# A norm vector's load and a weight split moved at two seams of a two-block transformer kernel on one Trainium2 core

## The reference, cut to what matters

```python
for i in range(DEPTH):                                   # DEPTH = 2
    h = rms_norm(x, norm1_g[i]) * (1.0 + sc1) + sh1
    x = x + g1 * attention_i(h)                          # begins with h @ w_in: (512 x 1024) @ (1024 x 3072)
    h = rms_norm(x, norm2_g[i]) * (1.0 + sc2) + sh2
    y = hierarchical_moe(h, ...)                         # each token: 2 of 32 experts, weighted
    x = x + g2 * y
x = rms_norm(x, final_norm_g)                            # final norm of the first block
# second block: h = x; for l in range(DEPTH): h = h + hybrid_mixer(rms_norm_2(h, norm_mix[l]), ...) ...
#   hybrid_mixer begins with xn @ w_in[l]
```

## Time and profile before

| | us |
|---|---|
| median of 3 runs (2644.32 to 2647.06) | 2645.24 |
| the profiled execution, whole | 2640.27 |
| its span, first to last instruction | 2638.2 |
| PE busy in it | 2262.7 |
| DVE busy | 1091.4 |
| ACT busy | 591.2 |
| POOL busy | 292.3 |

### The profile page before, as it was taken

The page is one execution under the profiler, slowest core; times in us unless marked ns, Lnnn a source line. Parts: engine busy times, 40 slices in busy tenths (PEclk is TensorE's granted clock), DMA queues, the critical chain, the costliest instruction groups (busy, mean ns, idle before and its releaser), DMA issues.

```text
span 2638.2 us, 34590 instructions
## 1 busy us (share of the span) xinstructions
PE 2262.7 (86%) x12932; PEld 1477.3 (56%) x12932; DVE 1091.4 (41%) x1953; ACT 591.2 (22%) x1157; POOL 292.3 (11%) x518
## 2 busy tenths in 40 slices
PE   4998686898977679996988887775998999999997
PEld 2874374453433368653554443343787765787764
DVE  2237744333333342654323233335327615227614
ACT  3114521000000031541000000003336214336213
POOL 0000111212121110000212122112000000000000
PEclk9999897999999989998999999997999799999799
DMA  6247827999999832115999999995211021121021
GB/s 243 96 154 312 344 100 312 420 420 420 419 420 420 354 138 98 64 80 227 368 420 419 419 419 419 420 419 225 78 71 64 1 112 42 64 85 65 1 80 40
DMA packets 132190, 611.73 MB, mean 232 GB/s; under 512 B 28164, under 2 KB 28198, under 8 KB 72314
## 3 DMA queue, kind: packets, MB, share of 16 engines
q1 hardware_dynamic: 117552, 591.28, 55.7%
q0 software_dynamic: 11456, 16.88, 1.8%
q10 hardware_dynamic: 3088, 2.27, 0.3%
HBM read 604.00 MB, written 26.26 MB: 239 GB/s over the span
## 4 chain that ended last, share of the span: by engine, by line
PE 60%; DMA 24%; DVE 10%; issue 2%; ACT 2%; ACTq 1%; SPq 1%; POOL 0%; DVEq 0%; POOLq 0%
DMA normed_by_feature<-in_expert_w_up 15%; PE banks L1292 9%; PE banks L1084 8%; PE banks L1086 8%; PE banks L1085 8%; DMA weight_ring<-in_expert_w_gate 6%; PE banks L1227 4%; PE banks L1310 4%; PE banks L1112 2%; DVE normed_by_token L2186 2%; PE banks L1459 1%; PE banks L1011 1%; DMA weight_ring<-in_sb_w_in 1%; PE banks L1273 1%; PE banks L1320 1%
## 5 line engine op out<-in xcount | busy, mean ns | idle before, releaser
L1292 PE MATMUL banks<-weight_ring,scratch 128*64 128x256 f32 x3264 | 386.8, 385 | 85.8 <-DMA weight_ring<-in_expert_w_gate 51.9
L1292 PEld LDWEIGHTS banks<-weight_ring,scratch 128*64 128x64 f32 x3264 | 228.6, 138 | 267.0 <-DMA weight_ring<-in_expert_w_gate 78.7
L1084 PE MATMUL banks<-weight_ring_rounded,scratch_rounded 128*128 128x512 f32 x704 | 278.7, 396 | 10.2 <-DVE ormed_by_feature_rounded L2047 3.6
L1086 PE MATMUL banks<-weight_ring_rounded,scratch_rounded 128*128 128x512 f32 x704 | 275.2, 391 | 0.0
L1085 PE MATMUL banks<-weight_ring_rounded,ormed_by_feature_rounded 128*128 128x512 f32 x704 | 275.0, 391 | 0.0
L2034 DVE TENSOR_TENSOR weight_ring_rounded<-weight_ring,weight_ring_rounded 128x4096 fp32r<-128x4096 f32 x26 | 115.0, 4425 | 231.5 <-ACT weight_ring_rounded L1558 231.5
L2372 DVE TENSOR_SCALAR scratch<-scratch 128x256 f32<-128x256 f32 x68 | 20.0, 294 | 347.5 <-ACT scratch L1754 347.5
L1084 PEld LDWEIGHTS banks<-weight_ring_rounded,scratch_rounded 128*128 128x128 f32 x704 | 132.8, 189 | 46.0 <-issue 11.6
L1754 ACT ACTIVATE scratch<-banks 128x256 f32<-128x256 f32 x68 | 26.1, 385 | 574.6 <-PE banks L1292 574.6
L1292 PE MATMUL banks<-normed_by_feature,scratch 128*64 128x256 f32 x1088 | 129.4, 383 | 29.5 <-DMA normed_by_feature<-in_expert_w_up 29.5
L1086 PEld LDWEIGHTS banks<-weight_ring_rounded,scratch_rounded 128*128 128x128 f32 x704 | 132.7, 189 | 28.1
(11 more groups left out here) (356 smaller groups left out, 3428.6 us busy)
## 6 DMA issues: line engine op xcount, KB each, us to landing
weight_ring<-in_expert_w_gate SPq DMA_DIRECT2D x136, 1024.0 KB, 26.2
weight_ring<-in_expert_w_up SPq DMA_DIRECT2D x68, 1024.0 KB, 27.0
weight_ring<-in_expert_w_down SPq DMA_DIRECT2D x68, 1024.0 KB, 27.8
normed_by_feature<-in_expert_w_up SPq DMA_DIRECT2D x68, 1024.0 KB, 27.8
normed_by_token<-in_expert_w_down SPq DMA_DIRECT2D x68, 1024.0 KB, 27.3
weight_ring<-in_ada_w SPq DMA_DIRECT2D x20, 2048.0 KB, 12.4
weight_ring<-in_w_in SPq DMA_DIRECT2D x12, 2048.0 KB, 8.2
weight_ring<-in_diff_w_in SPq DMA_DIRECT2D x6, 2048.0 KB, 8.9
```

The lines of the kernel that those rows point to most:

```text
L1084: pe.matmul(out_ap, left_high, right_high, start=i == 0, stop=False)
L1086: last = pe.matmul(out_ap, left_high, right_low, start=False, stop=i == KD - 1)
L1292: last = pe.matmul(PS[ROWS * half:ROWS * (half + 1), 1 + n // 2, 0:HIDDEN // 2], XGT[:, j, h, :], w[:, j, HIDDEN // 2 * half:HIDDEN // 2 * ...
```

## The change

Three edits. The norm vector of the final norm is loaded by SP at the start of the second layer's expert stage, behind its wait for `blocks_ready` and a wait for the last reader of the buffer, and no longer behind the loads of rows. DVE no longer makes the low part of the first unit of "qkv" 1 and "project" 0. POOL makes it, in two halves of 128 x 2048 values: the first (chunks 0 to 3) at the start of stage "combine", as soon as ACT's high part is there; the second (chunks 4 to 7) behind the root of tile 3, with a semaphore of its own (`first_unit_low`) for which TensorE waits.

```diff
+LOW_BY_POOL = (("qkv", 1), ("project", 0))
...
-        plan[-1].units_before = sum(stage.units for stage in plan[:-1])
+        plan[-1].units_before = sum(stage.units for stage in plan[:-1]) - sum((stage.kind, stage.arg) in LOW_BY_POOL for stage in plan)
...
                 if stage.kind == "final" and stage.arg == 0:
-                    sp.dma_start(GB[:, 0, :], final_norm_g.partition_broadcast(P)).then_inc(gain_in, 16)
                     load_early(stage_of("project", 0), [1])
...
                     sp.wait_ge(blocks_ready, layer + 1)
+                    if layer == DEPTH - 1:
+
+                        residual_wait(sp, stage)
+                        sp.dma_start(GB[:, 0, :], final_norm_g.partition_broadcast(P)).then_inc(gain_in, 16)
...
-                    pe.wait_ge(unit_low, stage.units_before + i + 1)
+                    if (stage.kind, stage.arg) in LOW_BY_POOL and i == 0:
+                        pe.wait_ge(first_unit_low, LOW_BY_POOL.index((stage.kind, stage.arg)) + 1)
+                    else:
+                        pe.wait_ge(unit_low, stage.units_before + i + 1)
...
+            def unit_low_chunks(stage, i, chunks):
+
+                u, width = stage.load + 2 * i, unit_width(stage, i)
+                loaded_wait(pool, u + 1)
+                return pool.tensor_tensor(rounded_slot(u, width)[:, chunks, :], slot(u, width)[:, chunks, :], rounded_slot(u + 1, width)[:, chunks, :].bitcast(F32), ALU.subtract)
...
+                if stage.kind == "combine":
+                    unit_low_chunks(next_product(stage), 0, slice(0, KD // 2))
...
                     for t in range(T):
                         pool.wait_ge(sumsq_ready, stage.scaled + t + 1)
                         rstd(1, D, 1e-6, rstd_ready, t)
+                    if (stage.kind, stage.arg) in (("norm", ("first1", 1)), ("final", 0)):
+                        unit_low_chunks(next_product(stage), 0, slice(KD // 2, KD)).then_inc(first_unit_low, 1)
...
-                    unit_low_half(next_product(stage), 0)
                     for t in range(T):
                         dve.wait_ge(rows_back[t], 32 * (layer + 1))
```

More of the change, by code:

```diff
@@ L444, in build_program @@
         unit_low = semaphore("unit_low")
+        first_unit_low = semaphore("first_unit_low")
         mod_stored = [semaphore(f"mod_stored{n}") for n in range(2)]
```

## The result

The changed kernel takes 2649.09 us (median of 20 runs, 2646.80 to 2653.65) against 2644.97 (20 runs) of the kernel before: ratio 1.002, 95% interval 1.0014 to 1.0027, so 3.7 to 7.1 us slower; the medians differ by 4.1 us, which is 0.16% and under the 0.2% that the forecast had taken as the line between the same and slower. Forecast were 2651.9 us in a range of 2645.0 to 2656.0, and +6.65 us as the sum. The direction held, the size was too large by 2.5 us. Two executions fell far out, one of the kernel before beside the first experiments (3020.87 us) and one of the experiment with the second half behind the norm (6793.32 us; the median of its others is 2645.86), and the ratios leave them out.

A forecast was written before the change was run, and what follows sets the result against it. The prediction took the chains of waits inside two seams as what counts, with PE busy behind them. First seam +4.65, second +1.4, gather +0.4, clock +0.2 gave +6.65 on 2645.24, so 2651.9 us, range 2645.0 to 2656.0.

The forecast's parts named there:

- the two engines pass each other: Both seams: two-input DVE operations keep 1.28 us beside POOL, so -4.2 us, 2641.0 us; chance 0.07.
- The slow rival: Both seams: POOL takes 5.65 us for each half, each +1.15, so +11.2 us, 2656.5 us; chance 0.13.
- The sign of being wrong: Forecast wrong if tile 3's norm kept its length, or if the blend of tile 0 started at 923.7.
- GpSimd first behind the root: Behind tile 3's root, POOL's second half needs no semaphore of the root and starts ahead of DVE's norm, which waits 4.5 us.
- The norm at the first seam is held: Tile 3's one-input norm, bounds 0 and 4.5 us, taken as held 4.5 because its rate suggests more than one path.
- Front of the first seam: Tile 0's blend starts when POOL's first half ends, 925.2 to 925.3 against 925.12 to 925.2: +0.15 us.
- Front of the second: Up to tile 3's root: early vector 3.35 us sooner, less 0.15 for the blend and 0.1 for roots meeting norms: -3.1 us.
- The block: Behind tile 3's root at each seam, DVE's norm stands behind POOL's second half: +4.5 us each.
- Behind the block: After tile 3's norm, DVE's evacuations and low chunks and PE's eight turns, so all products, wait; nothing subtracted.
- The clock: Turns of tile 3 follow a hole, so PE's clock may rise later: 0 to 1.4 us for both seams, taken 0.2.
- The gather: Layer 1's first gather of block rows, 3.54 us, shares DMA with the vector's 512 KB: 0 to 1.3 us, taken 0.4.
- DVE first: DVE's norm goes ahead of POOL's second half behind tile 3's root: first seam +1.75, second -1.05, 2646.3 us; chance 0.16.

The follow-up runs named there:

- the probe: Changed kernel plus a VectorE memset, sum and copy under GpSimd's first half at the first seam; sum 1.22 us, copy 3.12 us, no whole time given.
- the split alone: Changed kernel with the norm vector's load back behind the loads of rows, so only GpSimd's two halves: 2652.05 us, ratio 1.0021 against the kernel before.
- its own kernel: Changed kernel, but GpSimd's second half waits until VectorE has finished tile 3's norm: 2646.10 us, ratio 1.000 against the kernel before.

## Why the prediction was right, and where its sum was off

- **The rival "the two engines pass each other" fell, the forecast's mechanism held.** Blends, final norms and the doubled-rate norm were all held by GpSimd's half.
- **GpSimd's rate** (4.5 us a half): the four halves took 4.489 to 4.507 us. The slow rival (5.65) fell. The Trainium skill's 4497 ns (GPSIMD Engine Reference, "Performance versus the Vector engine") agrees with the trace.
- **The sign of being wrong.** The forecast called itself wrong if tile 0's blend started at 923.7. It is read as started 5.05 us behind the first load of rows, which is 923.87 in the times of before, as its rows landed. But it did its work only behind GpSimd's half: the sign was badly chosen, since a held operation shows its start and not its wait. Its length (2.39 us) is what tells.
- **GpSimd first behind the root**: yes, and with more margin than argued. Its operation was read as started 0.02 us before the root's end, VectorE's 0.04 after it.
- **The norm at the first seam is held**, taken from its rate alone: 4.98 us, and the probe's copy is held the same way, while a sum at the single rate isn't.
- **Front of the first seam**, +0.15: tile 3's root ends 20.83 us behind the first load in after, 20.97 in before, -0.14. The step that failed: I let the blend start afresh at GpSimd's end. The held operation has been started already, and ends 1.1 us behind GpSimd in place of 1.28.
- **Front of the second**, -3.1: measured 21.89 against 25.28, -3.39. The same, and 0.1 us for a meeting of roots and norms that cost nothing.
- **The block**, +4.5 at each: +4.23 and +4.24. From the root's end to the norm's end it is 5.02 and 5.56 us against 0.79 and 1.32. Again the start of the held instruction is in the shade.
- **Behind the block**, nothing subtracted: this is the term that was missed. In before, TensorE was still turning the last chunks of tiles 0 to 2 when tile 3's norm was done, and from the norm's end to ScalarE's first evacuation it took 1.45 us (first seam). In after these turns fall into the hole: 949.01 - 948.44 = 0.57 us. That takes back 0.88 us at the first seam and 0.57 at the second (1.14 to 0.57). It holds in all traces: at the 16 seams at which tile 3's norm isn't held, the first evacuation comes 3.07 to 3.14 us behind the end of tile 2's norm, though tile 3's norm ends anywhere from 0.82 to 1.46 us ahead of it.
- **The clock**, +0.2: it rose later, in the products, as forecast. In before it rose with the last turns, at 942 and 1833. In after it stayed at half through all turns and the first products, at both seams:

```profile
951.00:954.00 3.00, 2.69 (x6) 0.50 0.00 0
954.00:955.00 1.00, 1.00 (x5) 0.75 0.00 0
...
1843.00:1845.00 2.00, 1.25 (x4) 0.50 0.00 0
1845.00:1848.00 3.00, 3.00 (x8) 0.50 0.00 0
1848.00:1850.00 2.00, 2.00 (x8) 0.80 0.00 0
```

  At the first seam this cost nothing in the end: the first product came 3.21 us later than in before, the tenth 4.13, the 25th 3.21 again. At the second the first came 0.28 us later, the tenth 1.62, the 28th and all behind it 0.69, so 0.41 us stayed. Products ran at half clock for some 3.2 us at the first and 4.6 us at the second. What made up for the rest is a point that the forecast had wrong: behind the seams PE was not "busy without gaps" in before, but waited between the first products for the parts of the chunks (6.77 us busy of the 8 from 1835 to 1843), and slower products fill these gaps.
- **The gather**, +0.4: 3.74 against 3.54, and over the kernels 3.63 to 3.90 (six traces, mean 3.73) with the vector at that place, 3.48 to 3.55 (five traces, mean 3.51) without. 0.2 us, and nothing when the load is issued ahead of the wait.

In sum: first seam -0.14 + 4.23 - 0.88 = 3.21, second -3.39 + 4.24 - 0.57 + 0.41 = 0.69, gather 0.20: 4.1 in place of 6.65. The estimate for the rival "DVE first" (+1.1 us) was borne out by its own kernel: +1.44, -0.80 and +0.13, 0.8 us, and a ratio of 1.000.

What stays open: that the late clock costs 0.4 us at the second seam and nothing at the first is read from two traces, not tried by itself, and why it rose sooner behind the first seam isn't known; and where the 3.8 us between the two profiled executions ahead of the first seam came from, and the 0.6 us outside the seams and the gather behind it.

## What to carry to other kernels

Before work is moved from VectorE to GpSimd, look at what VectorE does while GpSimd would run: here its two-operand and doubled-rate operations didn't run beside a GpSimd operation on SBUF, so the moved work stayed in VectorE's time at half the speed (4.5 us a half in place of 2.28), and an order within a tenth of a microsecond decided who stood. A hole of the receiving engine is no gain if the other one needs the same path; cutting the work to fit VectorE's own holes where it waits for loads was the better way, but a small one: it shortened the two seams by 4.0 to 4.9 us together, of which the early vector alone is 3.4, and whole times can't tell the rest. A step that ends sooner brings nothing while another one beside it ends later, as TensorE's turns did here. And a block isn't to be priced by its length alone: ask what else was late behind it, since that now lies in its shade.

## What had not been expected of the hardware

- GpSimd's next instruction, where it needs no semaphore, was read as started 0.02 us before the one ahead had ended (943.40 against 942.88 + 0.54). In all six places with this order (after, the split alone and the probe, two seams each) VectorE, which waited for the first, came 0.06 to 0.07 us behind it.
- A held VectorE operation ended 0.5 to 1.1 us behind GpSimd, less than its own length: 0.54 for the norm of 0.75, 1.1 for an addition or a final norm of 1.28.
- Two GpSimd operations back to back are no closed wall: one VectorE addition slipped in between and the two took 9.92 us, where 2 x 4.5 are 9.0.
- In the kernel with the second half behind the norm, TensorE's clock fell back to half while PE stood still behind the turns (granted 1.00 up to 1836, 0.50 from 1837), though it had just risen.
